# A two-block transformer step on one core: the context branch's norm, projections and key norms set among the selection's turns, its scan directions in eight pieces, and roots taken of 16 columns

## What is computed

```
def peer(h, w_query, sub_keys, expert_u, expert_v):          # per token and head
    sv, si = lax.top_k(sc, PEER_TOPK)                         # 16 of 128, twice
    top_s, top_j = lax.top_k(cand_s, PEER_TOPK)               # 16 of the 256 pairs
    gate = softmax(top_s)
    act = gelu(einsum('tnd,td->tn', expert_u[et], xt)) * gt
    return einsum('tn,tnd->td', act, expert_v[et])

def rwkv_scans(r, k, v, w_lo, a_lo, lp, init):
    kk = to_heads(k * lp["k_k"])
    kk = kk * lax.rsqrt(jnp.maximum(jnp.sum(kk * kk, axis=-1, keepdims=True), 1e-24))
    for d in range(2):                                        # forward, backward
        decay = exp(-DECAY_SCALE * sigmoid(w0[d] + tanh(w_lo) @ w_up[d]))
        a = sigmoid(a0[d] + a_lo @ a_up[d])
        k_d = k * (1 + (a - 1) * k_a)
        state, y = wkv_scan(init[d], r, decay, kk, kk * a, v, k_d, reverse=(d == 1))

hc = modulate(rms_norm_2(ctx, norm1_g), csh1, csc1)
_, ctx_states = mixer_block(hc, lp, zeros, need_output=False)
hx = modulate(rms_norm_2(x, norm1_g), sh1, sc1)
out_x, _ = mixer_block(hx, lp, ctx_states, True)              # ends in a norm per head
```

## Time and profile before

| | |
|---|---|
| median of three runs | 1698.53 us |
| the profiled execution | 1703.35 us, of which its span, first to last instruction, 1701.8 us |
| PE, DVE, ACT, POOL busy | 1299.1, 947.3, 415.3, 335.7 us |
| TensorE's mean granted clock | 0.903 of 2.4 GHz |
| moved by DMA | 412.32 MB, of which 297.35 MB by POOL's queue (q0) |
| expert rows | 256, issued between 334.2 and 1077.8 us |

### The profile page before, as it was taken

How to read it: one execution, slowest core, us unless ns; L and a number is a source line. 1 busy time by engine, 2 the same in 40 slices (tenths; PEclk the granted TensorE clock), 3 DMA queues, 4 the chain that set the end, 5 groups by cost and what they waited for, 6 DMA issues and landing times. The chain is left out here.

```text
span 1701.8 us, 26012 instructions
## 1 busy us (share of the span) xinstructions
PE 1299.1 (76%) x10974; PEld 835.6 (49%) x10974; DVE 947.3 (56%) x2055; ACT 415.3 (24%) x1052; POOL 335.7 (20%) x315
## 2 busy tenths in 40 slices
PE   7979898945555555847876885479987777799997
PEld 6468765820111011523543552037887773688843
DVE  2967755538888886357557655320555334355511
ACT  2012300122222224134344332221343210111100
POOL 1000011124444444323443443100000000000000
PEclk9988998977887877968998998689999989899998
DMA  9443397799999999967997999623300021344442
GB/s 372 161 174 120 109 330 281 234 326 420 420 419 420 417 413 398 304 251 300 394 402 294 408 383 369 281 74 118 130 9 3 4 101 50 111 149 148 152 158 86
DMA packets 112293, 412.32 MB, mean 242 GB/s; under 512 B 10648, under 2 KB 35744, under 8 KB 78896
## 3 DMA queue, kind: packets, MB, share of 16 engines
q0 software_dynamic: 44576, 297.35, 44.0%
q1 hardware_dynamic: 62720, 104.38, 17.8%
q10 hardware_dynamic: 4880, 8.92, 2.3%
HBM read 408.51 MB, written 2.12 MB: 241 GB/s over the span
## 5 line engine op out<-in xcount | busy, mean ns | idle before, releaser
L1274 PE MATMUL psum<-arena 128*32 128x512 f32 x1024 | 304.4, 736 | 241.5 <-ACT arena L1262 221.3
L493 PE MATMUL psum<-actT,weights 128*128 128x256 f32 x1824 | 404.6, 385 | 5.2 <-ACT actT L606 2.3
L1233 POOL DMA_INDIRECT arena<-in_experts,arena x256 | 305.7, 1194 | 475.4 <-PE psum L1274 394.5
L493 PEld LDWEIGHTS psum<-actT,weights 128*128 128x128 f32 x1824 | 351.1, 193 | 58.0 <-ACT actT L606 5.6
L1274 PEld LDWEIGHTS psum<-arena 128*32 128x32 f32 x1024 | 56.2, 124 | 439.6 <-ACT arena L1262 286.7
L1246 DVE CUSTOM_DVE_ANT_0 arena<-arena 128x1024 f32<-128x1024 f32 x128 | 153.9, 1223 | 65.7 <-DMA arena<-in_experts,arena 55.9
L1246 DVE CUSTOM_DVE_ANT_0 arena<-normed,arena 128x1024 f32<-128x1024 f32 x128 | 153.2, 1222 | 42.9 <-DMA arena<-in_experts,arena 39.5
L1252 ACT ACTIVATE arena<-arena 128x2 f32<-128x2 f32 x128 | 26.0, 203 | 408.4 <-DVE arena L1246 394.6
L1625 PE MATMUL psum<-arena 64*64 64x64 f32 (+1 forms) x2816 | 82.2, 222 | 15.2 <-DVE arena L1742 7.1
L1625 PEld LDWEIGHTS psum<-arena 64*64 64x64 f32 x2816 | 77.7, 135 | 21.9 <-issue 12.4
L503 PE MATMUL psum<-weights,actT 128*128 128x512 f32 x192 | 84.7, 602 | 1.0 <-ACT actT L606 1.0
(11 more groups left out here) (353 smaller groups left out, 1554.5 us busy)
## 6 DMA issues: line engine op xcount, KB each, us to landing
weights<-in_w_in SPq DMA_DIRECT2D x18, 2048.0 KB
arena<-in_ada_wT POOLq DMA_DIRECT2D x48, 512.0 KB, 5.7
weights<-in_ffn_w_up SPq DMA_DIRECT2D x22, 1024.0 KB
weights<-in_ffn_w_down SPq DMA_DIRECT2D x5, 2048.0 KB
weights<-in_w_out SPq DMA_DIRECT2D x4, 2048.0 KB
weights<-in_w_peer_q SPq DMA_DIRECT2D x4, 2048.0 KB
arena<-in_experts,arena POOLq DMA_INDIRECT x256
weights<-in_w_ple_gate SPq DMA_DIRECT2D x2, 2048.0 KB
```

The costliest lines, as they stand in the source:

```text
L493: mm = nc.tensor.matmul(out[:, c * T:(c + 1) * T], w[:, k, c * P:(c + 1) * P], act[:, k, :], start=(k == 0), stop=(k == kc - 1))
L1233: nc.gpsimd.indirect_dma_start(out=rows[:, n % RING, :], out_offset=None, in_=dram["experts"], in_offset=bass.IndirectOffsetOnAxis(ap=eidx ...
L1274: mm = nc.tensor.matmul(SUMS[part, i, :], diag[:, pos, :], rows[:, pos, D + 512 * i:D + 512 * (i + 1)], start=first, stop=last, skip_group ...
```

## The change

**The order.** Norm, projections and key norms of the context leave the tail of the list and are put, one piece a turn, from turn 10 on beside the selection's pieces; `ctx_in` has 17 pieces with 6 matmuls each, `scan_common` 5. A direction has 8 pieces, and how many steps of each engine go into one is written in a tuple. Behind each pair of chunks stands an empty piece. The list still has 119 entries. To make room, the selection's spreads go to PSUM banks 6 and 7, which the context's transposes use as well (they therefore wait for the first two spreads alone), and the normed context lies where the keys were.

**The roots.** `head_rows` multiplies the squares, as the stationary side, by a matrix of two columns, so that tokens stand on the partitions and the eight heads of two token blocks in 16 columns (`per_head`). Maximum, root and reciprocal work on 128 x 16. `heads_over_rows` brings the result back over the 64 partitions of each head by 16 matmuls with the identity, into PSUM, and the last multiplication reads it there. Both scans and the norm per head after the second use it.

```diff
         def pe_scan_common(pe, m, t):
...
             pe.wait_ge(S(t + "sq_kk"), 1)
+            head_rows(m.roots, m.e).then_inc(S(t + "kk_pe"), 1)
             for j in range(TB):
                 for c in range(RC):
                     mm = nc.tensor.transpose(m.wide[1][:, j * 512 + c * P:j * 512 + (c + 1) * P],
                                              m.v[:, c, j * P:(j + 1) * P], K("ident"))
             mm.then_inc(S(t + "vt_pe"), 1)
-            for i in range(2):
-                mm = nc.tensor.matmul(m.wide[0][:, 512 * i:512 * (i + 1)], K("head_mean"),
-                                      m.e.rearrange("p c t -> p (c t)")[:, 512 * i:512 * (i + 1)], start=True, stop=True)
-            mm.then_inc(S(t + "kk_pe"), 1)
-            yield
+            yield
+            yield
+            yield
+            pe.wait_ge(S(t + "kk_dve"), 2)
+            heads_over_rows(m.roots).then_inc(S(t + "kk_pe"), 1)
+            yield
+
+        def head_rows(dst, src):
+            for b in range(TB):
+                for c in range(RC):
+                    at = 2 * (RC * b + c)
+                    mm = nc.tensor.matmul(dst[:, at:at + 2], src[:, c, b * P:(b + 1) * P], K("head_mean2"), start=True, stop=True)
+            return mm
+
+        def heads_over_rows(dst):
+            for b in range(TB):
+                for c in range(RC):
+                    for h in range(2):
+                        at = 2 * (RC * b + c) + h
+                        mm = nc.tensor.matmul(dst[HD * h:HD * (h + 1), c * T + b * P:c * T + (b + 1) * P],
+                                              per_head[:, at:at + 1].to_broadcast([P, HD]), K("ident"), start=True, stop=True)
+            return mm
...
         def act_scan_common(act, m, t):
-            act.wait_ge(S(t + "kk_max"), 1)
-            nc.scalar.activation(m.e, m.e, ACT.Sqrt).then_inc(S(t + "kk_rt"), 1)
+            act.wait_ge(S(t + "kk_dve"), 1)
+            nc.scalar.activation(per_head, per_head, ACT.Sqrt).then_inc(S(t + "kk_rt"), 1)
...
         def dve_scan_common(dve, st, m, t):
-            nc.vector.tensor_scalar(m.e, feat(m.wide[0]), float(HD), 1e-24, ALU.mult, ALU.max).then_inc(S(t + "kk_max"), 1)
+            nc.vector.tensor_scalar(per_head, m.roots[:, 0:16], float(HD), 1e-24, ALU.mult, ALU.max).then_inc(S(t + "kk_dve"), 1)
...
-            st.link(nc.vector.reciprocal(m.e, m.e))
-            st.link(nc.vector.tensor_tensor(m.kk, m.kk, m.e, ALU.mult))
+            nc.vector.reciprocal(per_head, per_head).then_inc(S(t + "kk_dve"), 1)
+            yield
+            dve.wait_ge(S(t + "kk_pe"), 2)
+            nc.vector.tensor_tensor(m.kk, m.kk, feat(m.roots), ALU.mult).then_inc(S(t + "kk_dve"), 1)
...
         def dve_direction(dve, st, m, t, d):
-            dve.wait_ge(S(t + "exp"), n_exp * (d + 1))
+            dve.wait_ge(S(t + "exp"), n_exp * d + 2)
...
         def pe_ctx_in(pe):
-            pe.wait_ge(S("eidx_ok"), QUARTERS * TB)
-            pe.wait_ge(S("gates_done"), QUARTERS * TB)
+            pe.wait_ge(S("eidx_ok"), SPREAD_BEFORE)
+            pe.wait_ge(S("gates_done"), SPREAD_BEFORE)
...
-                        if n % 12 == 0:
+                        if n % 6 == 0:
                             yield
...
         def pe_x_in(pe):
-            all_of(pe_scan_common(pe, x_m, "x"))
+            common = pe_scan_common(pe, x_m, "x")
...
+            for _ in range(4):
+                next(common)
             next(direction)
+            all_of(common)
             pe_features(pe, "x_r", actT)
+            pe.wait_ge(S("xkk_dve"), 3)
...
         def pe_y(pe):
-            head_means([GV[:, 0:512], GV[:, 512:1024]], m.cum, "gn_var")
-            out_steps(pairs[3:TB * RC])
+            head_rows(GV, m.cum).then_inc(S("gn_var"), 1)
+            out_steps(pairs[3:TB * RC - 2])
+            pe.wait_ge(S("gn_sq"), 2)
+            heads_over_rows(GV).then_inc(S("gn_var"), 1)
+            out_steps(pairs[TB * RC - 2:TB * RC])
...
+            def direction(d):
+                return dict(pe=lambda e: in_turns(pe_direction(e, m, t, d), (1, 0, 0, 0, 0, 0, 3, 2)),
+                            act=lambda e: in_turns(act_direction(e, m, t, d), (1, 1, 2, 2, 0, 0, 3, 2)),
+                            dve=lambda e, st: in_turns(dve_direction(e, st, m, t, d), (1, 2 + d, 2, 2, 2, 2, 1, 2)),
+                            pieces=8)
...
-        beside += [dict(act=act_ctx_norm, dve=dve_ctx_norm, pieces=1),
-                   dict(pe=pe_ctx_in, act=act_ctx_in, dve=dve_ctx_in, pieces=7)]
-        beside += list(scan_stages(ctx_m, "c"))
+        early = [dict(act=act_ctx_norm, dve=dve_ctx_norm, pieces=1),
+                 dict(pe=pe_ctx_in, act=act_ctx_in, dve=dve_ctx_in, pieces=17)]
+        scan = list(scan_stages(ctx_m, "c"))
+        early.append(scan.pop(0))
+        turn = SELECT_EVERY * (SPREAD_BEFORE - 2) + SELECT_PIECES
+        for f in early:
+            for k in range(f["pieces"]):
+                pieces[turn].append((len(beside), k))
+                turn += 1
```

More of the change, by code:

```diff
@@ L421, in build @@
         sgate = Region(after_rows - 3072).take(2048).rearrange("p (b n) -> p b n", b=TB)
-        ctx_m.tiles, ctx_m.wide = ("ctx_k", "ctx_lora", "ctx_v"), G
+        ctx_m.tiles, ctx_m.wide, ctx_m.roots = ("ctx_k", "ctx_lora", "ctx_v"), G, G[0]
         x_m.tiles = ("x_k", "x_lora", "x_v")
         x_m.wide = [AUX[:, 2 * i:2 * i + 2, :].rearrange("p i n -> p (i n)") for i in range(2)]
+        x_m.roots = G[tile_at["x_v"] % 2]
         x_back = Scan()
@@ L591, in pe_turn, with copy_turned @@
                 mm.then_inc(S("turn_pe"), 1)
-        def copy_turned(eng, tag, banks, gain, shift, dst, odd):
-            for i in range(odd, DC // 2, 2):
+        def copy_turned(eng, tag, banks, gain, shift, dst, odd, which=None):
+            for i in range(odd, DC // 2, 2) if which is None else which:
                 eng.wait_ge(S("turn_pe"), so_far(tag, DC // 2, i + 1))
@@ L1002, in score_bank @@
             return 2 * (quarter % 2) + b
-        SPREAD = {what: PS[:, 2 * (tile_at["ctx_k"] % 2) + i, 0:HEADS * PK] for i, what in enumerate("eg")}
-        FIRST_E = AUX[:, 0, 0:HEADS * PK]
+        SPREAD = {what: AUX[:, 2 + i, 0:HEADS * PK] for i, what in enumerate("eg")}
+        FIRST = {"e": AUX[:, 0, 0:HEADS * PK], "g": PS[:, 2 * (tile_at["ctx_k"] % 2), 0:HEADS * PK]}
         assert tile_at["ctx_k"] == tile_at["peer_q2"] + 2
@@ L2169, in one, with in_turns @@
             def one(pe, act, dve, pieces, *a, joined=(), rest=0):
-                return dict(pe=lambda e: pe(e, m, t, *a), act=act and (lambda e: whole_pieces(act(e, m, t, *a))),
-                            dve=lambda e, st: whole_pieces(dve(e, st, m, t, *a)), pieces=pieces, joined=joined, rest=rest)
-            yield one(pe_scan_common, act_scan_common, dve_scan_common, 2)
+                return dict(pe=lambda e: pe(e, m, t, *a), act=act and (lambda e: act(e, m, t, *a)),
+                            dve=lambda e, st: dve(e, st, m, t, *a), pieces=pieces, joined=joined, rest=rest)
+            def in_turns(steps, counts):
+                for n in counts:
+                    for _ in range(n):
+                        next(steps, None)
+                    yield
+            def direction(d):
[3 more added lines that the diff above has]
+                            pieces=8)
+            yield one(pe_scan_common, act_scan_common, dve_scan_common, 5)
             for d in range(2):
-                yield one(pe_direction, act_direction, dve_direction, 5, d)
+                yield direction(d)
                 for j in range(TB):
-                    yield one(pe_pair, act_pair, dve_pair, 3 + SOLVE_LEVELS, d, j)
+                    yield one(pe_pair, act_pair, dve_pair, 3 + SOLVE_LEVELS, d, j, rest=1)
             yield one(pe_chain, None, dve_chain, NCH)
+        SPREAD_BEFORE = 2
         def select_stage(b, quarter):
@@ L2197, in build @@
                 pieces[SELECT_EVERY * i + k].append((i, k))
-        beside += [dict(act=act_ctx_norm, dve=dve_ctx_norm, pieces=1),
-                   dict(pe=pe_ctx_in, act=act_ctx_in, dve=dve_ctx_in, pieces=7)]
-        beside += list(scan_stages(ctx_m, "c"))
+        early = [dict(act=act_ctx_norm, dve=dve_ctx_norm, pieces=1),
[7 more added lines that the diff above has]
+                turn += 1
+            beside.append(f)
+        assert turn <= len(pieces)
+        n_first = len(beside)
+        beside += scan
         beside += [dict(pe=pe_ple_proj, act=act_ple_proj, pieces=2, joined=(0,))]
```

71 lines of the change are left out of this document (52 added, 19 removed).

## The result

| | predicted | measured |
|---|---|---|
| time after, median | 1661.5 us (1648 to 1680) | 1670.56 us (1669.32 to 1672.01, 4 runs); before, beside it, 1697.49 |
| ratio to before | 0.978 | 0.9839, interval 0.9821 to 0.9857: 27 us faster |
| by the two profiled executions | 37.0 us | 1703.35 to 1671.55 us: 31.8 us |

A second set of runs on another chip gave 0.980 (0.9773 to 0.9828), 33 us by the medians; the kernel before takes 1690 us there. Times of different chips are therefore compared only by their ratio to before: a gain of an experiment over the changed kernel is the difference of the two ratios, taken of the time that the kernel before had beside it. The forecast, faster, was right; the gain was some 4 to 10 us smaller. The profiled execution of before had lain 4.8 us over the median then known, and the prediction let that of after lie as far over; it lay 1.0 over.

What follows compares the result with a forecast made beforehand. The ring of expert rows was bound by DMA, 5.07 us a turn, with 43.9 us lost to late engines. 36.4 gained there, less 2, plus 2.6 made 37.0: 1703.35 to 1666.4, as a median 1661.5 us (1648 to 1680).

Steps and rivals of the forecast that it cites:

- The valleys of before: Stretches from 656 us on where the DMA rate fell below 417 GB/s: 32.4 and 11.5 us, together 43.9, recoverable.
- Early part: Context work among 23 turns beside the selection: costs 0 to 6 us, taken as 1.
- low-clock rival: PE at 1.2 GHz in the 12 turns with projections: 9.3 us a turn, 13 us slower overall, 1712; chance 0.04.
- The token load's 8.3 us: Loss at 685 to 710 us while the next block's tokens, 2 MB, load beside the rows; the change leaves it.
- Direction 0: First direction in eight pieces: its first piece makes DVE 5.3 us late; priced at 1.5 us lost (0 to 5.3).
- direction 1: Second direction in eight pieces, beside the pairs of chunks: DVE at worst 6.3 us late; priced at 4 us (0 to 6.3).
- turn of the blocks: Turn 63, where DVE waits for PE to add up the block, now inside the first direction: 0 to 4 us, taken as 1.
- cover: How late a turn may be before the DMA engines run dry: 4 to 5 us, beside pairs of chunks 2 to 3.
- Table changes: Rival: each ACT table change drains the engine, 1.4 us beyond its load; gain only 21 us, 1677; chance 0.03.
- Second scan's key norms: Narrow roots behind the ring: DVE's saving worth 0, PE's path 2 us longer (0 to 4).
- Norm per head: At the end, from the mean's matmul to the next projection: 11.4 us instead of 14.0, 2.6 gained (0 to 4.5).
- The ring's end: The end of the ring of expert rows, with its two small projections: claimed unchanged, no gain or loss priced.

Runs made afterwards that it cites:

- pieces undone: The changed kernel with both directions in five pieces again instead of eight, and six empty turns at the list's end: ratio 0.9896, 1680.51 us.
- scan later: The changed kernel with DVE's scan of a direction one turn behind ACT's sigmoids, nine pieces instead of eight: ratio 0.9774, 1660.79 us.
- doses: The kernel before with one to four useless DVE scans of 2.29 us each in turns 14, 22, 32 and 46: ratio 1.0058, 1709.56 us.

## Why the prediction came out as it did

- *The valleys of before could be had, 43.9 us.* Right in kind: 31.0 were, and most of the rest is found in the named places.
- *Early part, 1 us.* Right, and rather 0: 417 GB/s. DVE is busy for 217.5 us where it was 212.0, 5.6 more; the 11 that were priced held 2.8 of waiting. PE keeps up with 6 projection matmuls a turn (12 records of 0.24 us each), and `ctx_lora` causes no wait. The signs named for it came only in part: DVE's share is 88% and not over 90, and PE's clock is 1.00 from 460 to 510 us, while the projections run, but 0.82 on the mean of 410 to 656. The low-clock rival is out:

```profile
496.18 2.86 PE L1881 MATMUL psum<-actT,weights 128*128 128x256 f32 x12
```

- *The token load's 8.3 us stay.* 7.4 did.
- *Direction 0, 1.5 us; direction 1, 4; turn of the blocks, 1.* This step was mis-sized: 4.3, 7.3 and 4.1, 9.2 us more than priced, and POOL's gap of 10.35 us at direction 0 is a sign that was to be absent. The mechanism, a late first piece against a cover, was the right one (pieces undone, scan later, doses); two sizes were off. The lateness was taken from DVE alone, 5.3 and up to 6.3; POOL was 7.7 and 7.4 late. At direction 0 PE's turn of 3.63 us added 1.7 to DVE's part, a duration that the earlier trace rows had shown (3.60) and that the prediction set against the cover but not against the lateness; at direction 1 PE's own queue made the wait 8.46. The cover was taken at 4 to 5 us and, beside the pairs, at 2 to 3; it was 3.4 and 0.1. The early part's and the tokens' smaller losses and some 2 us beside the pairs gave part of it back: 31.0 for 36.4. So the sum came near partly by luck: beside the pairs the changed kernel loses 5.0 us from 730 to 840 in one profile and none in the other, more than the 2 that helped here.
- *Table changes.* ACT goes on right behind the load in the directions too; the rival is out:

```profile
668.73 1.28 ACT L1562 ACT_TABLE_LOAD   x1
670.03 1.57 ACT L1562 ACTIVATE weights<-psum,small 128x256 f32<-128x256 f32 x4
```

- *Second scan's key norms, +2 us.* It was +4.4. `head_rows` at 1.92 is as priced; the low-rank matmuls, 3.78 for 2.00, and `heads_over_rows`, 2.75 for 1.9, were done at a granted clock of 0.55, in the middle of small matmuls and two waits of 1.30 and 1.19 us; it was 1.00 before. The price was right for the full clock: beside the selection `heads_over_rows` took 1.97 us.
- *Norm per head, -2.6 us.* It was 3.2, 10.8 us for 14.0 from the mean's matmul to the next projection:

```profile
1385.28 1.95 PE L1464 MATMUL psum<-const,arena 128*128 128x2 f32 x16
...
1396.09 4.47 PE L2031 MATMUL psum<-weights,actT 128*128 128x512 f32 x6 [2.37 <-DVE actT L2113]
```

  Behind the ring's end the change gained 0.8 us in all; predicted were 0.6.
- *The ring's end is unchanged.* Right, but with POOL's gap of 17.24 us it held 11 to 17 us that could be had, more than any other place that was left, and the prediction passed over it because the change did not touch it.

## What to carry to other kernels

How late a turn may be is not read from the depth of a buffer ring: measure it with a few doses of useless work, and in more than one place. Here a ring of four turns, 20.3 us, covered 1.3 to 2.7 us of each dose, 4.6 in one place and 0.1 in another. Where one engine computes what the next needs, put the consumer's piece one turn behind the producer's; and when a list of work grows or shrinks, look at what its last entry blocks before giving the gain to the part that was edited.

## What was not expected of the hardware

- A turn's four matmuls took 1.91 us or 3.0 to 3.6, and the longer time came after waits of 2 to 4 us as well as after 8.4. In the kernel before that was so for 26 of 42 turns beside the selection. Where a turn is late, PE can add 1.7 us to it.
- Two waits of 1.2 to 1.4 us among small matmuls went with a clock of 0.55 where `head_rows`, 16 records of two columns, stood between them (eight profiles of eight, 3.78 us for a group of 2.00), and with 1.00 where four records of 512 columns did.
- The kernel before took 1698.93 and 1700.93 us on two chips and 1689.75 and 1689.9 on two others. The changed kernel's ratio was 0.984 and 0.980, in intervals that just meet. Its stretch 730 to 840 us has 398 GB/s in the first profile and 418 in the second; kernels that are the same in that stretch had 401 and 400 on the two slower chips and 414 on the second profile's.
